# Output rows and probabilities split in row form and turned by transposing transfers, query projection two tiles ahead

## What is computed

```
u = rmsnorm(h)
gla, g_gate, (sq, sk, sv), s_gate = project(u, w_in, w_gate_up, b_gate)
o_gla, S = gla_branch(*gla, s0, gla_norm)            # S_t = diag(a_t) S_{t-1} + k_t v_t^T
o_swa = softmax([q k^T / 8 in a window of 128, sink]) v
out   = concat(o_gla * silu(g_gate), o_swa * silu(s_gate)) @ w_out
y     = rmsnorm(h + out)
```

## Time and profile before

| | us |
|---|---|
| median of 3 runs | 903.19 (903.15 to 903.64) |
| profiled execution, whole | 904.62 |
| its span, first to last instruction | 902.8 |
| granted TensorE clock, mean | 0.975 |

### The profile page before, as it was taken

The page is one execution under the profiler, slowest core; times in us unless marked ns, Lnnn a source line. Parts: engine busy times, 40 slices in busy tenths (PEclk is TensorE's granted clock), DMA queues, the critical chain, the costliest instruction groups (busy, mean ns, idle before and its releaser), DMA issues.

```text
span 902.8 us, 22427 instructions
## 1 busy us (share of the span) xinstructions
PE 881.7 (98%) x9066; PEld 616.0 (68%) x9066; DVE 687.9 (76%) x2223; ACT 383.0 (42%) x1008; POOL 77.5 (9%) x117
## 2 busy tenths in 40 slices
PE   7898999999999999999999999999999999999997
PEld 5884576675858576675858576675858676775775
DVE  5899678868787778868787777868777777876854
ACT  4564543435353443435353433534353533434411
POOL 0041010101010010101010000101010100101200
PEclk7999999999999999999999999999999999999976
DMA  9921002020110202020100202020200102020014
GB/s 376 379 95 71 1 2 94 2 94 1 47 50 1 94 1 95 2 95 1 64 32 6 89 2 95 2 94 1 92 5 25 71 2 94 2 74 25 3 71 155
DMA packets 15687, 56.55 MB, mean 63 GB/s; under 512 B 3746, under 2 KB 5210, under 8 KB 14561
## 3 DMA queue, kind: packets, MB, share of 16 engines
q1 hardware_dynamic: 15296, 55.05, 16.1%
q10 hardware_dynamic: 288, 0.07, 0.0%
HBM read 44.33 MB, written 10.78 MB: 61 GB/s over the span
## 4 chain that ended last, share of the span: by engine, by line
PE 88%; DVE 5%; issue 4%; DMA 2%; ACT 1%; POOL 0%; SPq 0%; POOLq 0%; DVEq 0%
PE bank L575 24%; PE bank L577 23%; PE bank L576 23%; PE bank L766 3%; PE bank L680 3%; PE bank L692 2%; PE bank L815 1%; PE bank L788 1%; PE bank L792 1%; PE bank L629 1%; PE bank L752 1%; DVE w_in_hi_lo L1758 1%; PE bank L803 1%; DMA w_out_hi<-in_w 1%; DMA x_rows<-in_xq 1%
## 5 line engine op out<-in xcount | busy, mean ns | idle before, releaser
L575 PE MATMUL bank<-u_hi,w_in_hi_lo 128*128 128x128 f16 (+1 forms) x1288 | 208.5, 214 | 3.6 <-DVE w_in_hi_lo L1758 2.8
L577 PE MATMUL bank<-u_hi,w_in_hi_lo 128*128 128x128 f16 (+1 forms) x1288 | 208.1, 214 | 0.0
L576 PE MATMUL bank<-u_lo,w_in_hi_lo 128*128 128x128 f16 (+1 forms) x1288 | 208.1, 214 | 0.0
L575 PE MATMUL bank<-w_in_hi_lo,u_hi 128*128 128x512 f16 (+3 forms) x528 | 176.5, 343 | 3.6 <-issue 3.6
L577 PE MATMUL bank<-w_in_hi_lo,u_lo 128*128 128x512 f16 (+3 forms) x528 | 176.5, 342 | 0.0
L576 PE MATMUL bank<-w_in_hi_lo,u_hi 128*128 128x512 f16 (+3 forms) x528 | 176.5, 342 | 0.0
L575 PEld LDWEIGHTS bank<-u_hi,w_in_hi_lo 128*128 128x128 f16 x1288 | 123.8, 98 | 16.3 <-issue 13.0
L576 PEld LDWEIGHTS bank<-u_lo,w_in_hi_lo 128*128 128x128 f16 x1288 | 123.6, 98 | 0.3
L577 PEld LDWEIGHTS bank<-u_hi,w_in_hi_lo 128*128 128x128 f16 x1288 | 123.6, 98 | 0.0
L575 PE MATMUL bank<-w_out_hi,ogT_hi 128*128 128x512 f16 x256 | 98.0, 383 | 0.5 <-DVE ogT_lo L1679 0.5
L576 PE MATMUL bank<-w_out_lo,ogT_hi 128*128 128x512 f16 x256 | 98.0, 383 | 0.0
(11 more groups left out here) (303 smaller groups left out, 1740.2 us busy)
## 6 DMA issues: line engine op xcount, KB each, us to landing
xT<-in_xT SPq DMA_DIRECT2D x16, 512.0 KB, 4.9
x_rows<-in_xq SPq DMA_DIRECT2D x16, 512.0 KB
flex<-in_w SPq DMA_DIRECT2D x4, 2048.0 KB, 10.3
flex<-in_xq SPq DMA_DIRECT2D x16, 512.0 KB, 4.0
out_y<-flex SPq DMA_DIRECT2D x16, 512.0 KB, 2.6
w_out_lo<-in_w SPq DMA_DIRECT2D x2, 2048.0 KB, 12.4
w_out_hi<-in_w SPq DMA_DIRECT2D x1, 2048.0 KB, 10.0
w_out_hi<-in_w SPq DMA_DIRECT2D x1, 1088.0 KB, 7.5
```

The source lines that it names most:

```text
L575: nc.tensor.matmul(out, a_hi, b_hi, start=start and i == 0, stop=False)
L576: nc.tensor.matmul(out, a_hi, b_lo, start=False, stop=False)
L577: mm = nc.tensor.matmul(out, a_lo, b_hi, start=False, stop=stop and i == last)
```

## The change

- For tiles 1 to 14 the probabilities stay in rows: `rows_hi` (ScalarE) and `rows_lo` (VectorE) write their float16 halves to `pr16`, and `turn_prob_rows` on SP moves them with a transposing transfer into `PT`, four per tile of 128x512 float16 (128 KB). `mask_older` then makes the masked copy. The transfer of units 2 and 3 waits for the `values` of units 0 and 1, whose place it takes.
- In the same tiles the output row is split in rows (`split_out` on ScalarE, the rest in `scale_rows` on VectorE) into `og_rows`, which lies in the buffer `xq`, and `turn_rows` on SP turns each half with a transposing transfer of 128x1024 float16 (256 KB). `out_proj` waits for both. The load of the next rows into `xq` waits for them too.
- Tiles 0 and 15 (`on_pe`) keep TensorE's transposes.
- `gqk` is computed for tile t+2 between `sg`(t+1) and the output projection of t. `bc`(t+2) opens the tile, the first scores stand after the first quarter of `sq`. The ring's order in the middle is bc(t+2), sq(t+1), sklow(t+1), gv(t+1), gg(t+1), sg(t+1), gqk(t+2).
- `scale_u`(t+2) stands early in the tile, `split_u`(t+2) of VectorE behind `take_z`, `final_scale` behind `scale_rows`, `residual` last. The norm of x is prepared three tiles ahead. A table load for SiLU stands explicitly behind `split_out`.

```diff
+def on_pe(n):
+    return n in (0, NT - 1)
...
+        og_rows = xq[:, :].bitcast(F16).rearrange("p (l c) -> p l c", l=2)
...
+        pj_filled = [(u, n, reader[u]) for u, n in (
+            ("bc", 0), ("sklow", 0), ("bc", 1), ("gqk", 0), ("sq", 0), ("sklow", 1), ("gv", 0), ("gqk", 1), ("sq", 1),
+            ("gv", 1), ("gg", 0), ("sg", 0), ("gg", 1), ("sg", 1), ("bc", 2), ("gqk", 2))]
+        for n in range(1, NT - 1):
+            pj_filled += [(u, n + ahead, reader[u]) for u, ahead in (
+                ("bc", 2), ("sq", 1), ("sklow", 1), ("gv", 1), ("gg", 1), ("sg", 1), ("gqk", 2))]
...
+            def turn_rows(t):
+                at_ring.wait_full(sp, "y1", t + -1)
+                for l, (dst, ready) in enumerate(((ogT_hi, (act_o, "hi1")), (ogT_lo, (dve_o, "gsc1")))):
+                    ready[0].wait(sp, ready[1], t)
+                    sp.dma_start(dst[:, :, :], og_rows[:, l], transpose=True).then_inc(og_turned, 16)
+            def turn_prob_rows(t, u):
+                if u >= 2:
+                    pe_pv.wait(sp, f"pv{u - 2}", t)
+                else:
+                    pe_pv.wait(sp, f"pv{u + 2}", t + -1)
+                sp.wait_ge(pr_split, prob_unit(t, u))
+                sp.dma_start(PT[:, u % 2, 0].rearrange("p l h c -> p (l h) c"),
+                             pr16[:, u % 2].rearrange("p l h c -> p (l h c)"), transpose=True).then_inc(pr_turned[u % 2], 16)
...
+                else:
+                    for u in range(4):
+                        turn_prob_rows(t, u)
+                    if t.n + 3 <= NT:
+                        load_xT(t + 3)
+                    turn_rows(t)
+                    store_y(t + -1)
+                    sp.wait_ge(og_turned, 32 * t.n)
+                    if t.n + 3 <= NT:
+                        load_xq(t + 3)
+                    load_xres(t)
...
                 if g == 0 and d0 == 0:
-                    tr.wait_freed(pe, "og1", t)
+                    if on_pe(t.n):
+                        tr.wait_freed(pe, "og1", t)
+                    else:
+                        pe.wait_ge(og_turned, 32 * t.n)
...
-                if not early:
-                    proj(nxt, "gqk")
-                    scores(t, 0)
-                    proj(nxt, "sq")
...
                 else:
+                    bc(t + 2)
+                    proj(nxt, "sq", between={0: [(first_scores, t)]})
+                    scores(t, 1)
                     proj(nxt, "sklow")
                     proj(nxt, "gv", 4)
-                values(t, 0)
-                values(t, 1)
-                if early:
                     leaf_scores(t)
-                turn_probs(t, 2)
-                turn_probs(t, 3)
-                if early:
-                    proj(t, "sg")
-                else:
-                    leaf_scores(t)
+                    values(t, 0)
+                    values(t, 1)
                     proj_rest(nxt, "gv", 4)
-                values(t, 2)
-                level_scores(t, "L1", 0)
-                values(t, 3)
-                level_scores(t, "L2", 2)
-                turn_keys(t)
-                turn_low(t)
+                    level_scores(t, "L1", 0)
+                    level_scores(t, "L2", 2)
+                    turn_keys(t)
+                    turn_low(t)
+                    values(t, 2)
+                    values(t, 3)
...
-                proj(nxt, "sg", 5)
-                turn_out(t, 0)
-                turn_out(t, 1)
-                proj_rest(nxt, "sg", 5)
-                out_proj(t, 0, 0, 5)
-                if not (t.static and t.off + 2 > NT):
+                if early:
+                    proj(nxt, "sg", 5)
+                    turn_out(t, 0)
+                    turn_out(t, 1)
+                    proj_rest(nxt, "sg", 5)
+                    out_proj(t, 0, 0, 5)
                     bc(t + 2)
-                out_proj(t, 0, 5)
-                out_proj(t, 1)
+                    out_proj(t, 0, 5)
+                    out_proj(t, 1)
+                    proj(t + 2, "gqk")
+                else:
+                    proj(nxt, "sg")
+                    proj(t + 2, "gqk")
+                    out_proj(t, 0)
+                    out_proj(t, 1)
             iterations(pe, body)
             t = Tile(NT - 1)
...
-                    tr.wait_full(act, "og1", t + -1)
+                if g == 0 and t.n > 0:
+                    if on_pe(t.n - 1):
+                        tr.wait_full(act, "og1", t + -1)
+                    else:
+                        dve_o.wait(act, "gsc0", t + -1)
+                if g == 1 and t.n > 0 and not on_pe(t.n - 1):
+                    dve_o.wait(act, "gsc1", t + -1)
...
+            def rows_hi(t, u):
+                if prob_unit(t, u) > 2:
+                    act.wait_ge(pr_turned[u % 2], turned_count(t, u) - 16)
+                act_w.wait(act, f"p{u}", t)
+                nc.scalar.activation(pr16[:, u % 2, 0], PR[:, u % 2], ACT.Identity, scale=P_TOP
+                                     ).then_inc(act_p.sem, 1)
...
+            def split_out(t):
+                dve_o.wait(act, "rscs", t)
+                for g in range(2):
+                    c = slice(g * 512, g * 512 + 512)
+                    nc.scalar.activation(og_rows[:, 0, c], gates[:, c], ACT.Identity, scale=amax[:, 1:2]
+                                         ).then_inc(act_o.sem, 1)
...
+                else:
+                    for u in range(2):
+                        probs(t, u)
+                        rows_hi(t, u)
+                    final_root(t + -1)
+                    take_sq(nxt)
+                    split_u(t + 2)
+                    for u in range(2, 4):
+                        probs(t, u)
+                        rows_hi(t, u)
...
+                else:
+                    split_out(t)
+                    nc.scalar.preload_act_table_set(SILU_SET)
                 take_gate(nxt, 0)
                 take_gate(nxt, 1)
                 nc.scalar.preload_act_table_set(LOG_EXP_SET)
                 decays(nxt)
...
+                else:
+                    take_qk(t + 2)
+                    if t.n + 3 <= NT:
+                        square_rows(t + 3)
+                        norm_rows(t + 3)
+                    final_square(t)
...
+            def rows_lo(t, u):
+                act_p.wait(dve, f"h{u}", t)
+                V.scalar_tensor_tensor(out=pr16[:, u % 2, 1], in0=PR[:, u % 2], scalar=P_TOP, in1=pr16[:, u % 2, 0],
+                                       op0=ALU.mult, op1=ALU.subtract).then_inc(pr_split, 1)
+            def mask_older(t, u):
+                dve.wait_ge(pr_turned[u % 2], turned_count(t, u))
+                V.tensor_tensor(PT[:, u % 2, 1].rearrange("p l h c -> p (l h) c"),
+                                PT[:, u % 2, 0].rearrange("p l h c -> p (l h) c"), bcast(older16[:, :], 1, 4),
+                                ALU.mult).then_inc(dve_p.sem, 1)
...
+                V.tensor_scalar(a[:, 1:2], a[:, 3:4], O_TOP, None, ALU.mult).then_inc(dve_o.sem, 1)
+                dve_o.wait(dve, "rscs", t)
                 for g in range(2):
-                    c = g * 512
-                    V.tensor_scalar(gates[0:n, c:c + 512], gates[0:n, c:c + 512], a[:, 3:4], O_TOP, ALU.mult,
-                                    ALU.mult).then_inc(dve_o.sem, 1)
+                    c = slice(g * 512, g * 512 + 512)
+                    if on_pe(t.n):
+                        V.tensor_scalar(gates[:, c], gates[:, c], a[:, 1:2], None, ALU.mult).then_inc(dve_o.sem, 1)
+                    else:
+                        act_o.wait(dve, f"hi{g}", t)
+                        V.scalar_tensor_tensor(out=og_rows[:, 1, c], in0=gates[:, c], scalar=a[:, 1:2],
+                                               in1=og_rows[:, 0, c], op0=ALU.mult, op1=ALU.subtract
+                                               ).then_inc(dve_o.sem, 1)
                 V.tensor_scalar(isc[0:n, :], inv[0:n, NG - 2:NG], a[:, 2:3], 1.0 / O_TOP, ALU.mult, ALU.mult
                                 ).then_inc(dve_o.sem, 1)
...
                 else:
                     row_max(t, 0)
                     row_max(t, 1)
-                take_sq(nxt)
-                take_pt(t, 0)
-                take_pt(t, 1)
-                row_max(t, 2)
-                row_max(t, 3)
-                if early:
+                    final_mean(t + -1)
+                    rows_lo(t, 0)
+                    rows_lo(t, 1)
+                    scale_u(t + 2)
+                    take_sq(nxt)
+                    row_max(t, 2)
+                    row_max(t, 3)
+                    mask_older(t, 0)
+                    mask_older(t, 1)
+                    rows_lo(t, 2)
+                    rows_lo(t, 3)
+                    take_kv(nxt)
+                    assemble_leaves(t)
                     sink_steps(t)
...
                 take_z(t)
...
+                else:
+                    split_u(t + 2)
...
+                else:
+                    final_scale(t + -1)
...
```

(49 more changed lines are left out.)

211 lines of the change are left out of this document (110 added, 101 removed).

## The result

| | before | after |
|---|---|---|
| median, runs beside each other | 903.17 (901.24 to 903.64) | 915.47 (913.16 to 919.24) |
| profiled execution, whole | 904.62 | 914.24 |
| its span | 902.8 | 912.4 |
| granted TensorE clock, mean | 0.975 | 0.979 |

After takes 1.0144 times the time of before, with a 95% interval of 1.0105 to 1.0184. The change makes the kernel slower, by some 12 us in the medians and 9.6 us between the two profiled spans.

The account below looks back on a forecast made before the run. TensorE was taken as the bound, working 50.36 of 50.40 us in a middle tile. Per tile -1.95 + 1.8 + 1.05 = +0.9, over 14 tiles +12.6, once +2.3: 903.2 becomes 918, eight-in-ten range 892 to 946.

Parts of the forecast that it names:

- likeliest case: Whole kernel: both waits as worked out and the transposing transfers hidden; 910 to 926 us, chance 0.50.
- What is removed: TensorE, middle tiles: eight transposes of probabilities and eight of output rows go, 1.95 us per tile.
- First stop: TensorE before `sklow`: waits for the bank of `bc`, released by `scale_u`; 1.8 us per tile with restart.
- Second stop: TensorE before `gqk`(t+2): waits for the bank of `gg`, released by ScalarE's first SiLU; 1.05 us per tile with restart.
- Transfers: Transposing transfers on SP's queue: 3 us each, hidden behind TensorE's other work, so they cost nothing.
- late cases: Transposing transfers land late: 1020 us at the load's price (chance 0.13), at least 1218 at a per-block price (0.06).
- Once: Start of tile 1: `bc`(3) waits for tile 3's norm, behind `take_qk`(2) on ScalarE; 2.3 us, between 1.5 and 3.
- Sum: Whole kernel: +0.9 us per tile, +12.6 for 14 tiles, with the one-time 2.3 us +14.9; 918 us.
- The gain stays: Rival: no wait before `sklow`, because the bank of `bc` is released in time; 893 us, chance 0.13.
- neither wait: Rival: TensorE waits neither before `sklow` nor before `gqk`(t+2); 878 us, chance 0.05.
- The clock falls: Rival: the new stops bring one fall of TensorE's clock per tile, 1.7 us each; 942 us, chance 0.11.

Follow-up runs that it names:

- e1: The changed kernel with `scale_u` moved ahead of the two `rows_lo` on VectorE; 891.78 us, 0.9883 of before.
- e2: The changed kernel with the SiLU table load moved ahead of the row splits on ScalarE; 904.91 us, 1.0037 of before.
- e6: e4 with eight transposes of a constant, results unused, between `sg` and `gqk` in each middle tile; 888.86 us, 0.9855 of before.
- e3: The changed kernel with both `scale_u` ahead of `rows_lo` and the table load ahead of the row splits; 880.31 us, 0.9769 of before.
- e7: e4 with `take_qk(t + 2)` ahead of `final_square(t)` on ScalarE in tile 0; 878.48 us, 0.9729 of before.
- e5: The changed kernel with the transfer of the output rows' high part made three times, one behind the other; 988.27 us in one run.
- e8: e7 with, in middle tiles, the output projection ahead of `gqk` and the norm of three ahead before `take_qk`; 953.11 us in one run.
- e4: e3 with, in tile 0, the norm of tile 3 ahead of `final_square`, `take_qk` and the residual; 880.4 us, 0.9769 of before.

## Why the prediction was right, point by point

918 was predicted for the median and 915.5 measured, inside the likeliest case's own range (910 to 926). Both stops are there, each released by the step that was named, and e1 and e2 show that each is what its order costs. The nearness of the total is partly luck: for the profiled execution the sum was 919.5 and 914.2 was measured, 5.3 us less, and the medians are closer only because the execution of after that was profiled lay 1.2 us below its median.

- **What is removed.** 1.95 us per tile, confirmed by e6 (0.87 for eight). The tile without any waits (e3) is shorter than before by 2.15; the step of 0.42 in place of 0.22 us at the start of each tile was not in the sum.
- **First stop.** 1.8 predicted with the restart, 1.76 idle and 1.84 from start to start measured. The chain was 6.5 and is 6.66, the cover 4.8 and is 4.9. The splits of probabilities from SBUF take 0.42 on ScalarE; from a bank they took 376 ns, which is the largest piece of the difference.
- **Second stop.** 1.05 predicted, 0.63 idle and 0.78 from start to start measured. Two terms were mis-sized. The one-column scale was to be ready 8.8 behind `gate_up` and is ready 8.4 behind it (511.03 to 519.43): VectorE takes 1.45 us from the start of `gate_window` to the update of the state, where before it took 1.69 with a short idle in it, and the `split_u` put ahead costs 0.1 less than thought. The row splits took 1.33, where I took 1.2 and 1.3 was the upper bound. -0.4 and +0.13 are the 0.27 that the stop is shorter. The load and the SiLU are as priced.
- **Transfers.** 3 us each predicted, 2.4 and 3.2 measured in the median, hidden in tiles 1 to 13; in tile 14 the second large one stopped TensorE for 0.2 us. The chance of 0.19 for late ones was the choice of price: the plain transfers were the right neighbours. In the late cases the working took 4.8 us of cover for a small transfer where its text has 4.5, so these come out some 4 us per kernel too low; nothing hangs on it. The Trainium skill (VectorE: DVE Perf Modes, "The three transpose paths") gives 1309 ns for one 128x128 block; the estimate made of it, that the blocks of one transfer follow each other at this price, did not come out: four blocks landed in 2.4 us and eight in 3.2. The other statement of the Trainium skill (Advanced Engine Details and Errata, "X-Bar Transpose (TRN2)"), as fast as plain ones, holds roughly in time from issue to landing: 3.2 us, beside 3.1 and 3.3 for plain ones. It does not hold by the byte, since these carry 512 KB and the transposed 256.
- **Once.** 2.3 predicted, 2.72 measured.
- **Sum.** Predicted per tile +0.9, measured +0.48: -2.15 + 1.84 + 0.78 = +0.47. The sum took both stops 14 times, but tile 14 has 0.8 us of the first and none of the second. For the spans 14.9 was predicted and 9.6 measured. By the starts of `gate_up`, the interval with the one-off stop grew by 3.9, the twelve behind it by 5.7 together, and the last shrank by 0.3. Prologue and tail together grew by 0.4 only. In the tail a new wait of 2.7 us for a DMA of the samples (L932) stands against a shorter fall of the clock, 3.4 us long where before had one of 10.2; that these nearly cancel was in no sum.
- **Rivals.** "The gain stays" was one edit away: e1 is at 891.8, where the rival had 893. With neither wait the prediction had 878; e3 is at 880.3 and e7 at 878.5. "The clock falls" didn't happen in after: the clock is 1.00 in tiles 1 to 13. Its one fall in tile 14 (3.4 us, from 829.9) has a counterpart in before, at 833.8, and is not of the two stops. e5 and e8 show that it would have with stops of 3.2 us.

What stays open is what makes the clock fall. The stop of 2.7 us at the start of tile 1 had no fall with it in after, e1 and e2, and had one in e3, e4, e5 and e6. No run separates what makes the difference. And just behind tile 14 it fell in before without any stop (last section).

## What to carry to other kernels

When work is taken off a full engine, count anew which bank each later product needs and what stands ahead of its release on the releasing engine: here two releases stood behind steps that they didn't need, and the stops of 23.6 and 8.1 us gave back more than the 27 us removed. The repair is cheap and is seen in the same rows: an engine idles just ahead of the unneeded step (0.86 us on VectorE, 2.79 on ScalarE), so the releasing step or a table load fits there. A transfer in place of a transpose is free only with cover: here about 2.4 to 3.2 us each, single ones up to 4.7, plus the issue on SP of the one ahead. Without cover it costs twice, in the stop and in the clock behind it. And a price checked by adding work (e6) is to be read tile by tile, since the total also holds a place where the added work fills a wait.

## What the runs showed of the hardware

A transposing transfer holds SP's queue for 1.2 to 1.3 us, against 0.33 to 0.47 for plain transfers of 512 KB. It is made of small packets. The pages of before and of after count them, and the last figures tell of packets under 512 B and under 2 KB:

```profile
DMA packets 15687, 56.55 MB, mean 63 GB/s; under 512 B 3746, under 2 KB 5210, under 8 KB 14561
```

```profile
DMA packets 75717, 71.22 MB, mean 78 GB/s; under 512 B 63777, under 2 KB 65241, under 8 KB 74592
```

These are 60,000 packets more for 14.7 MB more, and 14.7 MB is what the transposing transfers move (14 tiles of four times 128 KB and twice 256): some 245 bytes per packet. While the two large ones and a store are in flight, the DMA engines are busy throughout (share 1.06 in the window 488.00 to 491.21 of e8, with 255 GB/s). That other transfers are slower for it was not tested.

A stop of TensorE of some 3.2 us was followed, in 11 of the 13 tiles of e8 that had one of at least that length, by 3.4 us (once 6.8) at half the clock (1.2 GHz in place of 2.4), which cost 1.7 us per 3.4 (54.19 against 52.48 for a tile); a tile with two stops of 1.76 and 0.63 us had none.

A stop is not the only thing that a fall follows. In before the clock fell at 833.8, just behind tile 14, where TensorE had been busy throughout. What it did just ahead was the samples' projection, 120 matmuls of 8 columns. The windows view of the 3.4 us ahead and of those in the fall:

```profile
830.30:833.70 3.40, 3.40 (x110) 3.07 (x107) 1.03 (x6) 1.95 (x5) 0.63 (x4) 1.00 0.00 0
833.80:837.20 3.40, 3.40 (x27) 2.81 (x25) 3.33 (x18) 2.38 (x12) 1.84 (x2) 0.50 0.00 0
```
